# Six gate stages of a float32 transformer kernel: high weights meet the high and the low rows in one matmul of 512 columns, and VectorE adds the two halves

## What is computed

```python
# first block, and the second in the same way with mg = sigmoid(z['merge'])
merged = (mg[:, :, 0] * (y_a @ w_branch[l, 0])
          + mg[:, :, 1] * (y_b @ w_branch[l, 1])
          + mg[:, :, 2] * (y_c @ w_branch[l, 2]))
h = h + merged @ w_out[l]
```

## Time and profile before

| | |
|---|---|
| runs shown | 3459.1, 3461.1, 3470.57 us |
| profiled execution, its own time | 3463.11 us |
| its span, first to last instruction | 3460.6 us |
| TensorE busy | 2885.3 us (83% of the span) |
| GpSimd busy | 1686.3 us (49%) |
| ScalarE busy | 1189.2 us (34%) |
| VectorE busy | 1169.6 us (34%) |
| mean granted clock of TensorE | 0.91 |

### The profile page before, as it was taken

How to read it: one execution, slowest core, us unless ns; L and a number is a source line. 1 busy time by engine, 2 the same in 40 slices (tenths; PEclk the granted TensorE clock), 3 DMA queues, 4 the chain that set the end, 5 groups by cost and what they waited for, 6 DMA issues and landing times.

```text
span 3460.6 us, 52768 instructions
## 1 busy us (share of the span) xinstructions
PE 2885.3 (83%) x20704; PEld 2416.4 (70%) x20704; DVE 1169.6 (34%) x1616; ACT 1189.2 (34%) x1360; POOL 1686.3 (49%) x1290
## 2 busy tenths in 40 slices
PE   6999899898998987566776449877899988889898
PEld 1677688787898876322332148777789987879898
DVE  1487821124352333300000053366611234432335
ACT  1223333333544322201111124455544444444343
POOL 0000067676767765000000119654479975559897
PEclk8999999899999999688998669898999998889999
DMA  9432247375434767399999915433335543325443
GB/s 393 171 114 103 103 168 296 144 274 206 157 133 157 283 256 278 148 409 387 369 392 385 389 49 184 142 111 105 108 134 182 182 155 119 112 104 187 157 169 134
DMA packets 100898, 696.28 MB, mean 201 GB/s; under 512 B 11840, under 2 KB 15680, under 8 KB 17088
## 3 DMA queue, kind: packets, MB, share of 16 engines
q1 hardware_dynamic: 83088, 602.97, 46.6%
q10 hardware_dynamic: 15408, 74.85, 5.7%
q0 software_dynamic: 2272, 16.52, 1.2%
HBM read 774.25 MB, written 14.42 MB: 228 GB/s over the span
## 4 chain that ended last, share of the span: by engine, by line
PE 64%; DMA 13%; DVE 10%; ACT 7%; issue 3%; POOL 2%; SPq 1%; ACTq 1%; DVEq 0%; POOLq 0%
PE acc L569 51%; PE wk L569 10%; DMA ring<-in_moe 8%; DMA side_buf<-in_ada 2%; DMA stage<-in_ada 2%; ACT w_hi L1189 2%; PE acc L627 2%; POOL w_lo L542 2%; ACT L1189 1%; DVE yl L1729 1%; SPq L492 1%; DVE C_z L1732 1%; DVE rms_red L1741 1%; DVE C_sm L1729 0%; ACT hb L1189 0%
## 5 line engine op out<-in xcount | busy, mean ns | idle before, releaser
L542 POOL TENSOR_TENSOR w_lo<-stage,w_hi 128x512 fp32r<-128x512 f32 x1268 | 1668.7, 1348 | 1159.7 <-PE acc L569 615.3
L569 PE MATMUL acc<-xh,w_hi 128*128 128x256 f32 x3568 | 912.9, 294 | 29.9 <-DVE xl L1729 22.3
L569 PE MATMUL acc<-xl,w_hi 128*128 128x256 f32 x3568 | 899.6, 290 | 0.0
L569 PEld LDWEIGHTS acc<-xh,w_hi 128*128 128x128 f32 x3568 | 713.6, 200 | 73.3 <-issue 57.1
L569 PEld LDWEIGHTS acc<-xl,w_hi 128*128 128x128 f32 x3568 | 712.9, 200 | 0.7
L1189 ACT ACTIVATE w_hi<-stage 128x2048 fp32r<-128x2048 f32 x317 | 603.9, 1907 | 39.7 <-DMA stage<-in_main 35.3
L569 PE MATMUL acc<-xh,w_lo 128*128 128x256 f32 x3568 | 476.7, 287 | 0.0
L569 PEld LDWEIGHTS acc<-xh,w_lo 128*128 128x128 f32 x3568 | 452.2, 195 | 3.2 <-issue 2.3
L557 POOL DMA_DIRECT2D y_rows<-X_ysb x12 | 6.6, 552 | 560.4 <-ACT X_ysb L1189 560.4
L569 PE MATMUL acc<-h,stage 128*128 128x256 f32 x1024 | 233.8, 385 | 2.9 <-ACT h L1189 2.9
L569 PE MATMUL acc<-ring,xg 128*32 128x512 f32 x1024 | 150.0, 732 | 89.4 <-DMA ring<-in_moe 88.7
(11 more groups left out here) (455 smaller groups left out, 3641.3 us busy)
## 6 DMA issues: line engine op xcount, KB each, us to landing
stage<-in_main SPq DMA_DIRECT2D x317, 1024.0 KB, 4.8
ring<-in_moe SPq DMA_DIRECT2D x192, 1024.0 KB, 10.8
side_buf<-in_ada ACTq DMA_DIRECT2D x64, 1024.0 KB, 5.0
over_lo<-in_moe ACTq DMA_DIRECT2D x48, 1024.0 KB
over_hi<-in_moe ACTq DMA_DIRECT2D x42, 1024.0 KB
stage<-in_ada SPq DMA_DIRECT2D x32, 1024.0 KB, 8.6
stage<-in_sb SPq DMA_DIRECT2D x32, 1024.0 KB, 4.7
y_rows<-X_ysb POOLq DMA_DIRECT2D x11, 1024.0 KB, 9.8
```

Of the source, the lines that this page charges most:

```text
L542: last = pool.tensor_tensor(w_lo[:, k % 2, cs], stage[:, k, cs], w_hi[:, k, cs].bitcast(F32), ALU.subtract)
L569: return pe.matmul(o, w, r, start=start, stop=stop)
```

## The change

In the six gate stages `wide` gives way to `both`: xh and xl now lie in one tensor `xhl` (at the addresses that they had), and 16 matmuls of 512 columns, a run of 256 from each half, fill the whole bank. The 16 matmuls with w_lo add into its first half. VectorE then copies the first half to `sg` and adds the second half from PSUM to it, and ScalarE's sigmoid reads `sg` in place. Two semaphores order these steps: `sg_half` between VectorE's copy and its add, `sg_sum` from the add to the sigmoid. The wait for `sg_used` on ScalarE goes.

```diff
-    xh = sb("xh", [P, DT, T], F32R)
-    xl = sb("xl", [P, DT, T], F32R)
+    xhl = sb("xhl", [P, 2, DT, T], F32R)
+    xh, xl = xhl[:, 0], xhl[:, 1]
...
+        def both(k, q, t=None):
+
+            n = q * 4 + k
+            pe.wait_ge(hi_ready, n + 1)
+            pe.wait_ge(evac_done, n - 3)
+            for t in range(DT):
+                pe.matmul(acc[:, k, :], w_hi[:, k, t * P:(t + 1) * P], xhl[:, :, t, :], start=t == 0, stop=False,
+                          skip_group_check=True)
+            pe.wait_ge(lo_ready, n + 1)
+            for t in range(DT):
+                last = pe.matmul(acc[:, k, 0:T], w_lo[:, k % 2, t * P:(t + 1) * P], xh[:, t, :], start=False, stop=t == DT - 1,
+                                 skip_group_check=True)
+            last.then_inc(chunk_done, 1)
...
-        beside_ada("g_sb", 0, wide)
+        beside_ada("g_sb", 0, both)
...
-        each(pe, BASE["g_a"], 16, wide)
+        each(pe, BASE["g_a"], 16, both)
...
             def go(k, q, t):
                 def evac():
-                    if not (isinstance(t, int) and n0 + t < 2):
-                        act.wait_ge(sg_used, t + (n0 - 1))
+                    act.wait_ge(sg_sum, t + (n0 + 1))
                     kw = {} if b2 is None else {"bias": col("b2", t + b2)}
-                    fn(sg[:, k % 2, :], acc[:, k, 0:T], ACT.Sigmoid, **kw).then_inc(evac_done, 1)
+                    fn(sg[:, k % 2, :], sg[:, k % 2, :], ACT.Sigmoid, **kw).then_inc(evac_done, 1)
...
             def go(k, q, t):
+                dve.wait_ge(chunk_done, q * 4 + k + 1)
+                cp(sg[:, k % 2, :], acc[:, k, 0:T]).then_inc(sg_half, 1)
+                dve.wait_ge(sg_half, t + (m0 + 1))
+                tt(sg[:, k % 2, :], sg[:, k % 2, :], acc[:, k, T:2 * T], ADD).then_inc(sg_sum, 1)
                 dve.wait_ge(evac_done, q * 4 + k + 1)
```

More of the change, by code:

```diff
@@ L349, in build @@
     sg_used = nc.alloc_semaphore("sg_used")
+    sg_sum = nc.alloc_semaphore("sg_sum")
+    sg_half = nc.alloc_semaphore("sg_half")
     y_split = nc.alloc_semaphore("y_split")
@@ L801, in _ @@
         each(pe, BASE["p_s5"], 8, half)
-        beside_ada("g_s5", 1, wide)
+        beside_ada("g_s5", 1, both)
         each(pe, BASE["mlif"], 1, wide)
@@ L856, in _ @@
         each(pe, BASE["p_ml"] + 4, 4, half)
-        beside_ada("g_ml", 2, wide)
+        beside_ada("g_ml", 2, both)
         pe.wait_ge(mg_split, 1)
@@ L1106, in _ @@
         each(pe, BASE["p_a"] + 4, 4, half)
-        each(pe, BASE["g_a"], 16, wide)
+        each(pe, BASE["g_a"], 16, both)
         each(pe, BASE["p_b"], 8, half2)
-        each(pe, BASE["g_b"], 16, wide)
+        each(pe, BASE["g_b"], 16, both)
         base_d = BASE["fox"]
@@ L1159, in _ @@
         each(pe, BASE["p_c"] + 4, 4, half)
-        each(pe, BASE["g_c"], 16, wide)
+        each(pe, BASE["g_c"], 16, both)
         pe.wait_ge(mg_split, 2)
@@ L1956, in _ @@
         heads(dve, stage_a)
-        sg_n = [0]
+        sg_n = [0, 0]
         def merge_g(g, sg, pt, first=False):
-            n0 = sg_n[0]
+            n0, m0 = sg_n
+            sg_n[1] += 16
             def go(k, q, t):
+                dve.wait_ge(chunk_done, q * 4 + k + 1)
+                cp(sg[:, k % 2, :], acc[:, k, 0:T]).then_inc(sg_half, 1)
+                dve.wait_ge(sg_half, t + (m0 + 1))
+                tt(sg[:, k % 2, :], sg[:, k % 2, :], acc[:, k, T:2 * T], ADD).then_inc(sg_sum, 1)
                 dve.wait_ge(evac_done, q * 4 + k + 1)
```

## The result

The kernel after the change took **3437.9 us** (median of 4 runs, 3436.4 to 3441.4), against 3461.9 us before (median of 4, 3459.1 to 3470.6). The ratio is 0.9928, 95% interval 0.9909 to 0.9947: 24 us faster. I had forecast 3452.5, 8.6 us faster, with a range down to 3438.0. The direction was right, the size nearly three times the forecast. The profiled execution took 3438.94 us, its span is 3437.1.

The account below looks back on a forecast made before the run. TensorE was taken to bound the kernel, gate stages included, with GpSimd and side loads close behind. Terms -10.2 (plain stages), -4.0 (side-load stages) and +5.6 (ends) sum to -8.6 us: 3452.5 us against the 3461.1 median, range 3438 to 3472.

Parts of the forecast that it names:

- The fixed cost per matmul: Gate matmuls on TensorE: 13.3 ns fixed beyond the clocks, so 512 columns take 226.6 ns, saving 0.21 us per chunk.
- the rivals at 217, 240 and above: 512-column matmul: extra vanishes, 216.6 ns (chance 0.27); steady read pace, 240 ns (0.18); operand jump costs, above 240 (0.13).
- the jump: Moving operand of 512-column matmuls jumps 16 KB between halves; at 250 ns each, 3485 us; chance 0.13.
- The stages without side loads: g_a, g_b, g_c: 48 chunks at 0.21 us each, 10.2 us gained, with GpSimd hiding it.
- GpSimd: nothing charged for copy and add: VectorE's new copy and add do not slow GpSimd's w_lo; its 5.24 to 5.43 us stay under the 5.55 period.
- The side stages: g_sb, g_s5, g_ml: 10.2 us gained on TensorE less 6.2 for late side loads, net 4.0 us gained.
- the 1.05 us from chunk to issue: Side-load issue stands behind sigmoid and w_hi copy on ScalarE's queue, so it moves from 1.05 to 1.34 us after the chunk.
- a sign of being wrong: Side-load stages: landings growing longer because a shorter period packs the two streams of loads closer would count against the forecast.
- What is given back: Side-load stages: ten late loads cost 0.50 us more each, eight others 0.15 on average; 6.2 us in all.
- The ends: After g_sb, g_s5, g_ml, g_b, g_c the last sigmoid starts 1.12 us later: five times, 5.6 us lost.
- costed at nothing: Dropped sg_used wait, sigmoid from SBUF, unchanged tensor addresses, and loads and GpSimd pieces in the same order: 0 us.

Follow-up runs that it names:

- e6: The change, with the high and low halves of each row block stored side by side, one run of 512 columns: 3436.8 us, ratio 0.9934.
- e9: The kernel after the change, run once more unedited for a second profile: 3433.0 us, one run.
- e5: The change, plus fox's small row E_rm computed at the end of the head before, ahead of the loop's turn: 3433.9 us, ratio 0.9923.
- e7: The change, plus two one-column memsets on VectorE ahead of the row E_rm in every head of fox: 3447.0 us, ratio 0.9962.
- e1: The kernel before, with fox's row E_rm computed at the end of the head before, ahead of the loop's turn: 3436.5 us, ratio 0.9932.
- e8: The kernel before the change, run once more unedited for a second profile: 3470.1 us, one run.
- e2: The kernel before, with twelve unread one-column memsets on VectorE ahead of each of five gate stages: 3439.9 us, ratio 0.9958.
- e3: The change in g_a, g_b and g_c only, side-load gate stages as before: 3452.8 us, ratio 0.9982.
- e4: The change in g_sb, g_s5 and g_ml only, the other gate stages as before: 3455.4 us, ratio 0.9993.
- e10: e5 plus two one-column memsets on VectorE meant to precede the four products hb of the last RMS norm: 3430.8 us, ratio 0.9917.

## Why the prediction was right and wrong

**Right, in the mechanism and its size.** The fixed cost per matmul: 226.6 ns forecast, 227 measured, and the rivals at 217, 240 and above are out; e6 rules out the jump as well. The Trainium skill, "TensorE: Matmul & The Clock Gate", section "Back-to-back issue gap", would give 215.8 ns at 512 columns by the formula that I used. The page calls that the gap of an isolated matmul, and has about 131 ns for a stream of them at 512 columns. This trace agrees with neither: 227 is 11 more than the one and 96 more than the other. The stages without side loads: 10.2 forecast, 9.3 measured, since a chunk saves 0.19 and not 0.21. GpSimd: nothing charged for copy and add, and they did cost it nothing; a chunk stays at 5.23 and 5.42 us against the forecast's 5.24 and 5.43. Its pause in `g_b` is down to 0.08 us at the shortest.

**Right in size, in part by luck.** The side stages: 4.0 forecast; 2.1, 3.9, 4.5 and 3.6 in the change, e9, e5 and e7, and the same kernel twice differs by 1.0 to 1.8 here. The path was wrong: I read the 1.05 us from chunk to issue as ScalarE's queue and made it 1.34. It is TensorE's side step and 0.07 us, and the longer way to the sigmoid, 1.00 us, just fits into it, so the issue did not move. I had described that condition of `side_next` and left it out of the sum. In its place more loads were long: ten took over 5.9 us before and sixteen after, which I had named as a sign of being wrong. What is given back came out alike: 6.2 us forecast, 7.2 more waiting in the trace.

The ends: 1.12 each for five forecast, 5.6 us together. The sigmoid starts 1.00 after the last chunk (1237.89 to 1238.89 in `g_ml`). In the change `g_sb`'s end cost 0.7, `g_ml`'s 0.9, `g_b`'s 1.2 and `g_c`'s 1.0, and `g_s5`'s nothing: the stage behind it, `mlif`, is as long as before in every run, and in both chains TensorE goes on from `g_s5` into it without a wait for the gate's result, other than I had it. That is 3.8 us, and 1.8 less loss than forecast make up for most of 2.8 less gain.

**Wrong: the step "costed at nothing", by what it left unsaid.** The forecast was 8.6 us and the measurement 24. The step names the loads and pieces as the same ones in the same order, and the sum then takes for granted that every stage that is not edited keeps its length. I had `fox` in my rows for its product of 1.55 us, and the row of 1.37 us stood between them, starting 0.03 us behind GpSimd's piece: four times the 0.34 us that it takes alone, decided by 0.1 us. The change put two instructions per gate chunk into VectorE's program, the loop's turn became 0.11 us shorter, and six heads were each 1.13 to 1.16 us shorter on their path, 6.9 us, with some 4 on top that go with the clock. That was 11 of the 24 us. That these 11 us hang on the row's race is shown: e1 wins it in the kernel before and gains as much, e7 loses it in the change and `fox` is as long as before. Another 5 are `ple` (-1.5) and stages that move by several us between two executions of the same kernel (e8: +7.1).

**The range** reached to 3438.0 and the median is 3437.9. It was built from the gate stages' cases alone; a term for "a race elsewhere tips", 10 us either way, was in none of them.

## What to carry to other kernels

Before a change is costed, list the short instructions that last several times their usual time beside GpSimd, with their distance to the start of GpSimd's piece. Here it was 0.00 to 0.04 us where the race was lost, with one row at 0.01 ahead and still lost, and 0.07 to 0.10 ahead where it was won. At such distances an edit elsewhere, even one that computes nothing, can tip it (e2 did, e3 and e4 did not), and the gain of the edit must be measured with that race fixed one way (here e7 against the kernel before). Better is to take the instruction out of the race: e1 moved one row and gained as much as the change.

## What the runs showed of the hardware that was not expected

- The turn of VectorE's loop took 0.54 to 0.56 us in before, e3, e4 and e8, and 0.43 to 0.45 in the change, e2, e6 and e9, with the same instructions in the loop. Sixty memsets ahead of it are enough. What in the program's layout decides it stays open. So does `ple`, whose second chunk took 9.5 us in before, e1, e3, e4 and e8 and 8.0 in the change, e2, e5, e6, e7, e9 and e10.
- A VectorE instruction of 8 x 256 elements waits for a GpSimd piece as one of 128 partitions does: 0.34 us or 1.37 to 1.41. Where it comes first, the piece pays: 1.36 to 1.39 us in place of 1.26.
- Against a run of ready GpSimd pieces, a VectorE product of 1024 columns either waits for all of them (9.9 us) or takes turns (2.3 us), in two executions of one program.
- VectorE's gate products lasted longer in the change. In both kernels they start inside a GpSimd piece and end 0.28 us behind it; before, they start 0.77 us into the piece, and after, 0.40. In `g_a` and `g_b`, by lines of DVE, after:

```profile
L1744 DVE TENSOR_TENSOR G_sg<-G_sg,ptmp 128x256 f32<-128x256 f32 x14 | 17.0, 1211 | 11.2 <-ACT G_sg L1205 11.2
L1744 DVE TENSOR_TENSOR merged<-G_sg,ptmp 128x256 f32 x12 | 14.4, 1196 | 13.5 <-ACT G_sg L1205 13.5
L1753 DVE COPY G_sg<-acc 128x256 f32<-128x256 f32 x26 | 11.0, 425 | 92.5 <-PE acc L634 92.5
```

and before:

```profile
L1729 DVE TENSOR_TENSOR G_sg<-G_sg,ptmp 128x256 f32<-128x256 f32 x14 | 11.7, 833 | 95.7 <-ACT G_sg L1189 95.7
L1729 DVE TENSOR_TENSOR merged<-G_sg,ptmp 128x256 f32 x12 | 9.8, 817 | 59.3 <-ACT G_sg L1189 59.3
```

The mean of a product went from 817 or 833 ns to 1196 or 1211; the copy from PSUM is at 425. It cost nothing here, as VectorE has room.
